# An eleventh ring slot, and an expert's scatter moved behind the next expert's turning

## The reference, cut to what matters

```
def moe_ffn(h, router_w, router_b, wg, wu, wd):
    eidx, ew = route(h, router_w, router_b)        # top 2 of 16 experts, and their weights
    ...
    def expert_block(args):
        xb, e = args
        return (jax.nn.silu(xb @ wg[e]) * (xb @ wu[e])) @ wd[e]

    ys = lax.map(expert_block, (xs, blk_e)).reshape(P, D)
    out = jnp.zeros((T, D), jnp.float32).at[buf_t].add(ys.astype(jnp.float32) * buf_w[:, None])
    return out.astype(h.dtype)
```

## Time and profile before

| | |
|---|---|
| median of 3 runs | 1221.16 us |
| profiled execution, its own time | 1220.21 us |
| its span, first to last instruction | 1218.4 us |
| mean granted TensorE clock | 0.987 of full |
| PE busy | 1130.0 us, 93% |
| DVE busy / ACT busy | 357.8 us, 29% / 166.8 us, 14% |
| HBM read | 476.18 MB |
| DMA, mean over the span | 394 GB/s |

### The profile page before, as it was taken

One profiled execution on the slowest core, in us unless ns is written; L12 is line 12 of the kernel. 1 busy time (PEld: TensorE's weight loads), 2 busy tenths in 40 slices (PEclk: granted clock), 3 DMA queues, 4 the chain that ended last, 5 costly groups with the idle time before them and its releaser, 6 DMA issues.

```text
span 1218.4 us, 12360 instructions
## 1 busy us (share of the span) xinstructions
PE 1130.0 (93%) x5288; PEld 500.6 (41%) x5288; DVE 357.8 (29%) x729; ACT 166.8 (14%) x398; POOL 5.2 (0%) x8
## 2 busy tenths in 40 slices
PE   8998998899999999999999999999999999999995
PEld 3553554545344333333333337533333343333331
DVE  1559899763111211111111115211111111111113
ACT  1101233523000000000100006100000010000000
POOL 0000000000000000000000010000000000000000
PEclk9998999999999999999999999999999999999998
DMA  9998797984999999999999999899999999999993
GB/s 394 405 356 322 270 358 273 401 345 167 428 427 429 427 429 426 429 427 427 428 428 428 427 419 427 357 427 429 427 428 429 425 429 427 428 429 426 429 426 153
DMA packets 40153, 480.17 MB, mean 394 GB/s; under 512 B 5024, under 2 KB 6304, under 8 KB 8352
## 3 DMA queue, kind: packets, MB, share of 16 engines
q1 hardware_dynamic: 39040, 476.91, 93.9%
q10 hardware_dynamic: 1056, 2.43, 0.6%
HBM read 476.18 MB, written 1.05 MB: 392 GB/s over the span
## 4 chain that ended last, share of the span: by engine, by line
PE 82%; DVE 9%; DMA 6%; issue 2%; ACT 1%; DVEq 0%; ACTq 0%
PE ps L887 53%; PE ps L879 5%; PE ps L895 5%; DMA ring<-in_moe_wu 3%; PE ps L638 3%; DMA ring<-in_mod_w 3%; PE ps L738 2%; PE ps L641 2%; DVE work L1647 2%; DVE work L1651 1%; DVE ring L1309 1%; PE ps L903 1%; PE ps L579 1%; PE ps L701 1%; PE ps L644 1%
## 5 line engine op out<-in xcount | busy, mean ns | idle before, releaser
L887 PE MATMUL ps<-ring,tra 128*64 128x512 f32 x2048 | 446.7, 594 | 1.0 <-DMA ring<-in_moe_wu 1.0
L887 PEld LDWEIGHTS ps<-ring,tra 128*64 128x64 f32 x2048 | 144.1, 137 | 298.4 <-issue 295.7
L887 PE MATMUL ps<-ring,work 128*64 128x512 f32 x1024 | 228.7, 598 | 29.2 <-DVE work L1647 29.2
L887 PEld LDWEIGHTS ps<-ring,work 128*64 128x64 f32 x1024 | 83.2, 137 | 154.1 <-issue 117.3
L1642 DVE TENSOR_TENSOR work<-ps,work 128x512 f32<-128x512 f32 x32 | 22.1, 692 | 277.2 <-ACT work L1198 277.2
L1198 ACT ACTIVATE work<-ps 128x512 f32<-128x512 f32 x32 | 19.1, 597 | 533.5 <-PE ps L887 533.5
L895 PE MATMUL ps<-work,extra 64*128 64x512 f32 x256 | 63.6, 615 | 21.0 <-DVE work L1651 21.0
L1191 ACT ACTIVATE tra<-ps,cols 128x128 f32<-128x128 f32 x128 | 48.1, 456 | 240.2 <-PE ps L879 240.2
L1645 DVE TENSOR_TENSOR work<-work,ps 128x512 f32<-128x512 f32 x32 | 22.0, 689 | 181.7 <-PE ps L887 181.7
L879 PEld LDWEIGHTS ps<-extra,xn 128*128 128x128 f32 x512 | 61.0, 195 | 24.3 <-issue 22.7
L879 PE MATMUL ps<-extra,xn 128*128 128x128 f32 x512 | 66.9, 285 | 1.4 <-DVE extra L1555 1.4
(11 more groups left out here) (184 smaller groups left out, 712.4 us busy)
## 6 DMA issues: line engine op xcount, KB each, us to landing
ring<-in_moe_wg SPq DMA_DIRECT2D x64, 2048.0 KB, 23.9
ring<-in_moe_wu SPq DMA_DIRECT2D x64, 2048.0 KB, 23.4
ring<-in_moe_wd SPq DMA_DIRECT2D x64, 2048.0 KB, 23.0
ring<-in_mod_w SPq DMA_DIRECT2D x40, 1024.0 KB, 9.7
ring<-in_mod_w SPq DMA_DIRECT2D x4, 2048.0 KB, 18.5
ring<-in_attn_wqkv SPq DMA_DIRECT2D x4, 2048.0 KB, 11.2
ring<-in_attn_wo SPq DMA_DIRECT2D x2, 2048.0 KB, 10.9
ring<-in_tokens SPq DMA_DIRECT2D x2, 1024.0 KB, 16.3
```

The source lines that it names most:

```text
L887: last = mm(ps[SLOTS * h:SLOTS * h + SLOTS, b, :], lhs(k0 + k), w[:, k, h * NB:(h + 1) * NB], start=(k0 + k == 0), stop=(k0 + k == KT - 1) ...
```

## The change

Two things. **The ring** has RING = 11 slots instead of 10. The room comes out of SBUF that was reserved as scratch for dynamic DMAs, now 128 bytes (`dynamic_dma_scratch_size=128`); the new slot is number 10, and nothing of the attention stage lies in it. So unit 0 goes there at once: it is issued from LOADS at "ahead", between the modulation units 9 and 10, with no wait. The conditions of `slot_free` move on by one unit (what unit v waited for, unit v + 1 waits for), v = 10 takes slot 0, which v = 9 had, and later units wait for unit v - 11. **The scatter** of expert e - 1 stands in expert e behind `turn_hidden` and ahead of `turn_weights`; the wait for its ys_ready stands behind the up units. Only a layer's last expert (NE - 1) scatters at its own end too, behind its own down units.

```
-RING = 10
-FREE = (4, 8, 5, 9, 6, 7, 2, 3, 1, 0)
+RING = 11
+FREE = (10, 4, 8, 5, 9, 6, 7, 2, 3, 1, 0)
...
-LOADS = [("q", 0), 0, 1, ("v", 0), 2, "rows", 3, 4, ("k", 1), 5, 6, 7, 8, ("q", 1), 9, 10, 11, 12, ("v", 1), 13, 14, ("wo", 0),
-         15, 16, 17, ("wo", 1), "x", 18, 19]
+LOADS = [("q", 0), 0, 1, ("v", 0), 2, "rows", 3, 4, ("k", 1), 5, 6, 7, 8, ("q", 1), 9, "ahead", 10, 11, 12, ("v", 1), 13, 14,
+         ("wo", 0), 15, 16, 17, ("wo", 1), "x", 18, 19]
+AHEAD = 1
...
+            def slot_free(v):
+
+                if v < AHEAD:
+                    return
+                if v == 1:
+                    early_used(sp, ("v", 1))
+                elif v == 2:
+                    sp.wait_ge(sem("row_done"), 4)
...
+                elif v < RING:
+                    sp.wait_ge(sem("unit_used"), NA - RING + v + 1)
+                else:
+                    used(sp, v - RING)
...
+            def load_expert(layer, e):
+                for n in range(AHEAD if layer == e == 0 else 0, EU):
+                    load_unit(layer, e, n)
+
             for what in LOADS:
                 if what == "rows":
                     load_rows()
+                elif what == "ahead":
+                    for n in range(AHEAD):
+                        load_unit(0, 0, n)
...
+                if e:
+                    pe.wait_ge(sem("ys_ready"), q)
                 if pr_ + 1 < PAIRS:
                     pe.wait_ge(sem("sgat_ready"), PAIRS * layer + pr_ + 2)
                     gather(6, e2).then_inc(sem("gather_done"), 1)
...
                 turn_hidden().then_inc(sem("hT_turned"), 1)
+                if e:
+                    scatter(swT[(e - 1) % 2]).then_inc(sem("scattered"), 1)
                 if e + 1 < NE:
...
-                pe.wait_ge(sem("ys_ready"), q + 1)
-                scatter(swT[e % 2]).then_inc(sem("scattered"), 1)
+                if e == NE - 1:
+                    pe.wait_ge(sem("ys_ready"), q + 1)
+                    scatter(swT[e % 2]).then_inc(sem("scattered"), 1)
...
-    nc = bacc.Bacc("TRN2", target_bir_lowering=False, num_devices=1)
+    nc = bacc.Bacc("TRN2", target_bir_lowering=False, num_devices=1, dynamic_dma_scratch_size=128)
```

More of the change, by code:

```diff
@@ L465, in load_sum_unit, with load_unit @@
                     load(slot(2 + n % 2)[:, c0:c1], mod_w[layer, m][:, c0:c1], sem(f"sum_loaded_{n % 2}_{half}"))
+            def slot_free(v):
[5 more added lines that the diff above has]
+                    sp.wait_ge(sem("row_done"), 4)
+                elif v in (3, 4):
+                    sp.wait_ge(sem("scores_done"), NS)
+                elif v == 5:
+                    sp.wait_ge(sem("pv_done"), NS)
+                elif v == 6:
+                    sp.wait_ge(sem("oT_done"), 2 * TT)
+                elif v in (7, 8):
+                    sp.wait_ge(sem("half_summed"), 2 * (NSUM - 8 + v))
+                elif v < RING:
+                    sp.wait_ge(sem("unit_used"), NA - RING + v + 1)
+                else:
+                    used(sp, v - RING)
+            def load_unit(layer, e, n):
+                v = first_unit(layer, e) + n
+                slot_free(v)
+                s, _ = ring_slot(v)
+                src = (moe_wg, moe_wu, moe_wd)[n // 2][layer, e, (n % 2) * HALF:(n % 2 + 1) * HALF, :]
+                load(slot(s).rearrange("p (k n) -> p k n", k=4), src.rearrange("(p k) n -> p k n", p=P),
+                     sem(f"ring_loaded_{s}"))
+            def load_expert(layer, e):
+                for n in range(AHEAD if layer == e == 0 else 0, EU):
+                    load_unit(layer, e, n)
             for what in LOADS:
@@ L475, in _ @@
                     load_sum_unit(what)
[L477 to L503, removed]
             def further_loads(layer):
```

## The result

The changed kernel takes 1206.7 us (median of 4 runs, 1205.62 to 1208.3) against 1220.06 us of before: a ratio of 0.9882, with an interval of 0.9865 to 0.9898. That is 14.4 us less by the ratio, clearly faster. The forecast was 1214, or -6.7 us: it had the direction, but less than half of the size, and 1206.7 lies under the range's lower end, 1210. The profiled execution took 1205.62 us, 14.6 less than that of before.

What follows compares the result with a forecast made beforehand. The prediction took the DMA's bytes at 427 GB/s, plus pauses and a tail, as the bound. Its terms -4.9, -3.0 and +1.2 gave -6.7 us, so 1214 us from the 1221.16 median; range for 8 in 10: 1210 to 1218.5.

Steps and rivals of the forecast that it cites:

- What bounds the kernel: Whole kernel: the end is the DMA's end plus a tail, total bytes at 427 GB/s plus pauses behind a full ring.
- The sum: Whole kernel: -4.9 (unit ahead) - 3.0 (second pause) + 1.2 (tail) = -6.7 us.
- costs nothing: Ring's room taken from the dynamic-DMA scratch: no cost, since the kernel issues no DMA from GpSimd.
- The unit ahead: From 292 us on the DMA has one unit fewer to load, eleven being loaded at the first pause: -4.9 us.
- Its placing in LOADS: Extra 2 MB load in the attention stage fits free DMA time: cost taken as 0, bounds 0 to 4.9 us.
- rival (d): Attention stage: the ahead load delays it by its whole 4.9 us, giving 1219; chance 0.07.
- The second pause: Start of layer 1: the DMA's pause goes whole with one slot more, -3 us (bounds -2.5 and -4.5).
- Rival (c): Start of layer 1: the second pause stays, the pooling band's issue perhaps blocking longer, giving 1217; chance 0.08.
- The tail: Last expert, behind the last up unit: 0.76 us of wait turn into 1.99 us of scatter, +1.2 us.
- Rival (a): Experts that wait for loads: the granted clock falls, one or two falls in the last expert, giving 1217; chance 0.14.
- (b): Tail: waits hold the clock at 1.2 GHz when the last unit lands, up to 16.6 us more, 1230; chance 0.05.
- Rival (e): Whole kernel: TensorE sets the time, as the chain's 82% suggests, giving 1165; chance 0.01.

Runs made afterwards that it cites:

- the slot with the fast place: Kernel before with the eleventh slot, small scratch and unit issued ahead, but the scatter at its old place: ratio 0.9982, -2.2 us.
- the fast place alone: Kernel before with only the 128-byte scratch, so the ring begins at byte 128 instead of 16384; ten slots, old order: ratio 0.9978, -2.7 us.
- the slow place: Changed kernel whole, but with a scratch of 32 bytes instead of 128, so the ring begins at byte 32: 1213.52 us, ratio 0.9945.
- the control: The kernel before run once more, unchanged: 1219.24 us (one run).

## Why the prediction was right, and where it was not

**What bounds the kernel** was right for the changed kernel: it ends with the DMA's bytes plus a tail. TensorE lives on the ring's lead, and where its waits for VectorE fell from 50.2 to 3.5 us, its waits for the ring's loads rose from 1.0 to 30.7. For the kernel before it was only half of the truth. There the two bounds lie so close that either one alone holds the time: the scatter alone gives 0.9997, the slot with the fast place 0.9982, the fast place alone 0.9978, and only both sides moved together give 14 us. The trace of before had it in it: TensorE waits for a load once, in the last expert, and for 1.0 us only. The sum had the scatter at +1.2, with next to nothing of its gain reaching the end, and the slot at -7.9. Taken one by one these prices are wrong. The slot's -4.9 reaches the end only with the scatter moved, and on top of slot and fast place the scatter is worth 0.0100, 12.2 us (0.9982 to 0.9882).

**The step that failed** is the one that I did not take as a step: "From 292 us on the DMA does the same work in the same order, one unit fewer". The work was the same but not its rate. The small scratch was in the sum as "costs nothing", with the reason that no DMA is issued from GpSimd; that it moves the ring, and with it the destination of every load, I did not look at. A term of nothing should have been one of -7.7 us, by the two kernels that differ in it alone (0.9945 and 0.9882, good to some 2.7 us). With it the sum would have been -14.4.

The profiled pair has 7.9 us. Of these 1.5 come from an earlier end of the attention stage (first expert at 288.16 at the slow place, at 286.70 in the changed kernel). That part isn't shown to be the place's: the first packet behind the first pause came at 291.1 to 294.2 us in the kernels at a fast place, and at 292.1 to 294.4 in those at a slow one. Of the rest the packets' mean time would give 5.0: 3.5 ns, 8 packets for each engine and unit, 179 units from the pause to the last up unit. Their spacing tells more, 5.9. Between 300 and 700 us each engine has such a packet every 613.1 ns at the slow place and every 609.0 ns in the changed kernel, 4.1 ns apart. The pooling unit, whose packets have 1024 and 4352 bytes, accounts for 0.7: it took 8.45 us at the slow place and 7.75 in the changed kernel. Its packets differ too, 50.6 against 46.0 ns and 179.7 against 168.0. Together, 1.5, 5.9 and 0.7 are 8.1 us for the 7.9.

**The unit ahead**, -4.9, is -5.6 by the runs with and without the eleventh slot, at the fast place and with the scatter moved. That is its size, but together with whatever the slot does in the second pause. Its placing in LOADS was rightly put at no cost (VectorE waits 13.5 us in all for modulation units, before 14.3) but also brings nothing: rival (d) falls, and so does the reason for the placing.

**The second pause**, -3.0, was counted for the slot, and the slot alone doesn't give it. It was to let the DMA go on for one unit more, but with eleven slots the DMA also begins one unit further on, so from the first pause to the full ring in layer 1 it has 97 units to load either way. The run with the slot alone has a pause longer than before (share 0.30). It goes when TensorE also ends layer 0 earlier: slot and scatter together have 1.01 at the slow place and 1.02 at the fast one. The scatter with ten slots has 0.87 to 0.89, which the control shows without it. It is 4.5 us of mean idle time in the trace of before and 1.2 in the control (0.12 of 10 us), so what its end can bring differs by run. That the size came out is in part luck. In the profiled pair of before and the slow place the stream, from the first packet behind the first pause to the last unit's landing, takes 906.6 and 898.5 us: 8.1 less, 7.9 in the sum. The control's stream takes 903.9. Rival (c) falls: the pooling band's issue was blocked for 35.12 us now instead of 29.37, with no idle engine behind it:

```profile
666.84 3.20 SPq L419 DMA_DIRECT2D ring<-in_pool_w  x1
670.08 35.12 SPq L419 DMA_DIRECT2D ring<-in_band  x1
```

**The tail**, +1.2, was +0.8 in the profiled pair and +0.8 by the last down unit; taking it out gives nothing that can be measured.

**The clock.** Rival (a) happens, but where it costs nothing. Once in the stretch paced by the loads the granted clock falls, behind a wait of 2.0 us, with TensorE busy for 1.94 of 4 us; two down units take 8.77 us instead of 7.0 (1.7 us, as foretold), and the next waits for loads swallow it. Nor did the waits bring more falls: from 300 to 1190 us before has two (near 716 and 764 us) with one wait for a load, and the changed kernel two (near 367 and 1111 us) with 28. In the last expert, with 2.81 of 4 us busy, it stays at 1.00, its level of 2.4 GHz; so (b) falls:

```profile
1107.00:1111.00 4.00, 1.94 (x12) 0.45 (x8) 0.69 (x1) 0.60 (x1) 0.00 (x0) 1.00 1.04 438
1111.00:1115.00 4.00, 4.00 (x12) 1.25 (x14) 0.00 (x0) 0.00 (x0) 0.00 (x0) 0.57 0.98 418
...
1168.00:1172.00 4.00, 2.81 (x16) 0.97 (x16) 0.69 (x1) 0.60 (x1) 0.00 (x0) 1.00 1.02 438
1172.00:1176.00 4.00, 2.81 (x16) 0.79 (x14) 0.00 (x0) 0.00 (x0) 0.00 (x0) 1.00 1.02 430
```

**Rival (e)**, TensorE as the bound, fell with the bytes.

## What to carry to other kernels

Where two engines are nearly balanced, price an edit on either together with the other: alone each is worth nothing. When a kernel streams from HBM for most of its time, write down the rate of each packet class before and after, and read an edit of the SBUF layout (a scratch, a pad, a tensor's order) as an edit of where every load lands. Another 128 bytes in the start of a big landing buffer is a cheap thing to try: here the fast place was worth some 8 us of 1220 once the loads were the bound, and 2.7 when they were not.

## What the runs showed of the hardware

In the steady stream of loads a packet of 16384 bytes takes 611 ns nearly always if the ring begins at byte 128 or 16512 (mean 612.2), and mostly 611 to 622 ns if it begins at 32, 256, 8192, 16384, 16416 or 16448 (mean 615.8 to 616.0). The trace doesn't name a packet's engine. Followed from one packet's end to the next one's start, the slow and the fast packets alternate in the same chain, and seven chains of 505 or 507 packets between 330 and 640 us of before have means of 614.5 to 614.7 ns. So it isn't some engines that are slow. All slots of a ring are 16384 bytes apart, so every unit has the same offset from a multiple of 16384: 128 bytes is fast; 0, 32, 64, 256 and 8192 are slow. TensorE's reads of the ring have no part in it (615.8 ns without them), and for 15 to 20 us behind a long pause of the DMA 93 to 96% of the packets take 611 ns at a slow place too. Why 128 is the good one stays open: larger odd multiples of 128 (384, 640) were not tried, nor the place of the source in HBM. What the Trainium skill says of alignment (DMA: Bandwidth & Descriptors, How a descriptor splits into AXI transactions) is that a descriptor that doesn't start at a multiple of 256 bytes pays for the bytes ahead of it, which are fetched and not used; it speaks of reads. If it held for the destination too, the places 256, 8192 and 16384 should be no slower than 128. The packets' times say the reverse for the destination, 615.9 against 612.2 ns.
